# A macaron encoder trunk on one core: the first two weight units and x arrive in smaller pieces

## The reference

```python
def swiglu(x, w_gate, w_up, w_down):
    return (jax.nn.silu(x @ w_gate) * (x @ w_up)) @ w_down
...
    for l in range(DEPTH):
        x = layer_norm(ALPHA * x + FFN_RESIDUAL * swiglu(x, ffn1_w_gate[l], ffn1_w_up[l], ffn1_w_down[l]),
                       ln1_g[l], ln1_b[l])
        h = x @ w_in[l]
        ...
        x = layer_norm(ALPHA * x + mixed @ w_out[l], ln2_g[l], ln2_b[l])
        x = layer_norm(ALPHA * x + FFN_RESIDUAL * swiglu(x, ffn2_w_gate[l], ffn2_w_up[l], ffn2_w_down[l]),
                       ln3_g[l], ln3_b[l])
```

## Time and profile before

| | us |
|---|---|
| median of 3 runs | 986.75 |
| lowest and highest | 986.54, 987.31 |
| the profiled execution | 986.51 |
| its span, first to last instruction | 984.7 |
| PE matmul busy | 965.2 (98%) |
| DVE busy | 808.8 (82%) |
| ACT busy | 559.7 (57%) |
| mean granted TensorE clock | 0.997 |

### The profile page before, as it was taken

How to read it: one execution, slowest core, us unless ns; L and a number is a source line. 1 busy time by engine, 2 the same in 40 slices (tenths; PEclk the granted TensorE clock), 3 DMA queues, 4 the chain that set the end, 5 groups by cost and what they waited for, 6 DMA issues and landing times.

```text
span 984.7 us, 17315 instructions
## 1 busy us (share of the span) xinstructions
PE 965.2 (98%) x6744; PEld 892.4 (91%) x6744; DVE 808.8 (82%) x882; ACT 559.7 (57%) x611; POOL 21.1 (2%) x53
## 2 busy tenths in 40 slices
PE   6999999999999999999999999999999999999996
PEld 6999999899888999999989999998998889999996
DVE  5998887854888998887889988878469889988875
ACT  4655554557875655554565555544688656555543
POOL 1000000001000000000000000000010000000000
PEclk9999999999999999999999999999999999999998
DMA  8556645653244556454626684544624436645541
GB/s 332 215 207 243 240 171 172 214 214 129 92 162 156 201 202 226 171 215 172 239 80 221 213 298 171 213 172 171 214 87 164 152 155 214 226 169 216 173 154 43
DMA packets 33788, 184.14 MB, mean 187 GB/s; under 512 B 3792, under 2 KB 3792, under 8 KB 18640
## 3 DMA queue, kind: packets, MB, share of 16 engines
q1 hardware_dynamic: 32112, 173.55, 49.3%
q0 software_dynamic: 1488, 9.45, 2.3%
q10 hardware_dynamic: 144, 0.52, 0.1%
HBM read 182.46 MB, written 1.05 MB: 186 GB/s over the span
## 4 chain that ended last, share of the span: by engine, by line
PE 92%; DVE 5%; DMA 1%; ACT 1%; issue 0%; POOL 0%; DVEq 0%; SPq 0%; POOLq 0%
PE bank L1172 28%; PE bank L1173 28%; PE bank L1174 28%; PE bank L1301 7%; PE bank L1230 1%; DVE qT L869 1%; DVE soft_t L1058 1%; DMA raw<-stream 1%; PE bank L1484 1%; DVE xn L888 1%; DVE xT_lo L830 1%; DVE mx L1061 1%; DVE xn L856 1%; DVE w_lo L763 0%; DVE soft_t L1074 0%
## 5 line engine op out<-in xcount | busy, mean ns | idle before, releaser
L1172 PE MATMUL bank<-xT_hi,w_hi 128*128 128x256 f32 x1488 | 421.5, 283 | 0.0
L1174 PE MATMUL bank<-xT_hi,w_lo 128*128 128x256 f32 x1488 | 421.1, 283 | 0.0
L1173 PE MATMUL bank<-xT_lo,w_hi 128*128 128x256 f32 x1488 | 421.0, 283 | 0.0
L763 DVE TENSOR_TENSOR w_lo<-raw,w_hi 128x2048 fp32r<-128x2048 f32 x109 | 249.7, 2291 | 72.2 <-ACT w_hi L438 71.9
L438 ACT ACTIVATE w_hi<-raw 128x2048 fp32r<-128x2048 f32 x122 | 232.9, 1911 | 129.7 <-PE bank L1174 128.3
L1172 PEld LDWEIGHTS bank<-xT_hi,w_hi 128*128 128x128 f32 x1488 | 285.3, 192 | 3.9 <-issue 0.7
L1173 PEld LDWEIGHTS bank<-xT_lo,w_hi 128*128 128x128 f32 x1488 | 285.3, 192 | 3.0
L1174 PEld LDWEIGHTS bank<-xT_hi,w_lo 128*128 128x128 f32 x1488 | 285.3, 192 | 0.0
L1172 PE MATMUL bank<-w_hi,h_hi 128*128 128x512 f32 x284 | 111.4, 392 | 0.0
L1173 PE MATMUL bank<-w_lo,h_hi 128*128 128x512 f32 x284 | 111.4, 392 | 0.0
L1174 PE MATMUL bank<-w_hi,h_lo 128*128 128x512 f32 x284 | 110.5, 389 | 0.0
(11 more groups left out here) (151 smaller groups left out, 1197.4 us busy)
## 6 DMA issues: line engine op xcount, KB each, us to landing
raw<-stream SPq DMA_DIRECT2D x110, 1024.0 KB, 4.9
raw<-stream SPq DMA_DIRECT2D x108, 512.0 KB, 4.6
lnp<-ln_gb POOLq DMA_DIRECT2D x6, 1024.0 KB, 5.2
band<-rel_band POOLq DMA_DIRECT2D x2, 1024.0 KB, 9.1
xn<-x POOLq DMA_DIRECT2D x1, 1024.0 KB, 7.4
out<-xn SPq DMA_DIRECT2D x4, 256.0 KB, 2.0
qT<-xT SPq DMA_DIRECT2D x1, 512.0 KB, 4.9
qT<-xT ACTq DMA_DIRECT2D x1, 512.0 KB, 5.0
```

The source lines that it names most:

```text
L763: nc.vector.tensor_tensor(w_lo[:, at(slot)], raw[:, slot, :], w_hi[:, at(slot)].bitcast(F32), ALU.subtract).then_inc(lo_ready, 1)
L1172: nc.tensor.matmul(o, w[0], x[0], start=start, stop=False, skip_group_check=again)
L1173: nc.tensor.matmul(o, w[0], x[1], start=False, stop=False, skip_group_check=again)
L1174: return nc.tensor.matmul(o, w[1], x[0], start=False, stop=stop, skip_group_check=again)
```

## The change

Only the first two units of a layer's stream and the start of the program are edited.

- **Transfers.** SP no longer issues xT. It issues unit 0 as two quarters and a half (semaphores `quarter_ready`, `half_ready`, `raw_ready[0]`), and unit 1 as two halves (`u0_half_ready`, `raw_ready[1]`); this stands in the loop over layers, so it holds for both. ACT issues all of xT, as two quarters and a half, ahead of its table load.
- **Splitting.** ACT and DVE alternate between quarters of xT and of unit 0, then take unit 1 in halves, at the program's start. `first_hi` now counts three quarters and unit 1's first half there, so that the later phases wait for 4 where they waited for 1.
- **PE.** `first_two` replaces `first_columns` and the first `columns`: for each quarter of unit 0 and each half of unit 1 it runs high by high, low x, and low w. The count of real products is the same, 96. Before them, eleven products of the constant `neg_one` with itself (128x128, float32, into bank 3, which is overwritten later) run as soon as three constants are set.
- **A wait.** In the second feed-forward of layer 0, ACT waits for `quarter_ready` and `u0_half_ready` of the next layer before it splits that layer's unit 0.

```diff
-            sp.dma_start(qT[:, 0:4, :], xT_in[:, 0:4, :]).then_inc(xT_loaded[0], 16)
             sp.sem_inc(lo_ready, 3)
             with sp.Fori(0, DEPTH) as l:
-                for s in range(3):
-                    load(s, l * UNITS + s)
+                first = l * UNITS
+                sp.wait_ge(lo_ready, first + 1)
+                for c, ready in ((QUARTERS[0], quarter_ready), (QUARTERS[1], half_ready), (HALVES[1], raw_ready[0])):
+                    sp.dma_start(raw[:, 0, c], stream[first][:, c]).then_inc(ready, 16)
+                sp.wait_ge(lo_ready, first + 2)
+                for c, ready in zip(HALVES, (u0_half_ready, raw_ready[1])):
+                    sp.dma_start(raw[:, 1, c], stream[first + 1][:, c]).then_inc(ready, 16)
+                load(2, first + 2)
...
         def _(act):
+            for c, loaded_piece in zip((slice(0, 2), slice(2, 4), slice(4, 8)), xT_loaded):
+                act.dma_start(qT[:, c, :], xT_in[:, c, :]).then_inc(loaded_piece, 16)
             nc.scalar.preload_act_table(ACT.Silu)
             act.sem_inc(unit_used, 3)
-            act.dma_start(qT[:, 4:8, :], xT_in[:, 4:8, :]).then_inc(xT_loaded[1], 16)
...
                 if r < 3 * DEPTH - 2:
+                    if f == 1:
+                        act.wait_ge(quarter_ready, 16 * (l + 2))
+                        act.wait_ge(u0_half_ready, 16 * (l + 2))
                     split_hi(l, base + FFN_UNITS, 0, first[0] + FP, into=3, after=base + 3 * SF + 1)
...
+            for q, c in enumerate(QUARTERS):
+                part = slice(2 * q, 2 * q + 2)
+                act.wait_ge(xT_loaded[min(q, 2)], 16)
+                nc.scalar.activation(xT_hi[:, part, :], qT[:, part, :], ACT.Copy).then_inc(xhi_done, 1)
+                act.wait_ge((quarter_ready, half_ready, raw_ready[0], raw_ready[0])[q], 16)
+                nc.scalar.activation(w_hi[:, at(0, c)], raw[:, 0, c],
+                                     ACT.Copy).then_inc(hi_ready if q == 3 else first_hi, 1)
...
-                dve.wait_ge(first_hi, phase(l, p) + 1)
+                dve.wait_ge(first_hi, phase(l, p) + 4)
...
+                def all_three(slot, into, kcs, x_lo_at, w_lo_at):
+                    products(slot, into, kcs, w_hi, xT_hi)
+                    if x_lo_at:
+                        pe.wait_ge(xlo_done, x_lo_at)
+                    products(slot, into, kcs, w_hi, xT_lo)
+                    pe.wait_ge(*w_lo_at)
+                    return products(slot, into, kcs, w_lo, xT_hi)
+
+                for q in range(4):
+                    pe.wait_ge(xhi_done, q + 1)
+                    pe.wait_ge(*((hi_ready, 1) if q == 3 else (first_hi, q + 1)))
+                    last = all_three(0, bank[0], range(2 * q, 2 * q + 2), q + 1,
+                                     (lo_ready, split(0, 0)) if q == 3 else (first_lo, q + 1))
                 last.then_inc(unit_used, 1)
+                for half in range(2):
+                    pe.wait_ge(*((hi_ready, 2) if half else (first_hi, 4)))
+                    last = all_three(1, bank[7], range(4 * half, 4 * half + 4), 0,
+                                     (lo_ready, split(0, 1)) if half else (first_lo, 4))
+                last.then_inc(unit_used, 1)
...
+            def fill(count):
+                for i in range(count):
+                    plain(bank[3][:, 0:P], neg_one, neg_one, start=True, stop=True)
...
+            pe.wait_ge(consts, 3)
+            fill(11)
             pe.wait_ge(consts, 10)
```

65 lines of the change are left out of this document (26 added, 39 removed).

## The result

The changed kernel took **989.33 us** (median of 12 runs, 986.5 to 990.6) beside 986.75 of before (986.2 to 987.3 over 12 runs): a ratio of 1.0022, with a 95% interval of 1.0014 to 1.003. It is slower by 2.6 us by the medians and 2.2 by the ratio, where I forecast 1.1 us faster, and it lies outside my range. Its times also spread over 4 us, where before's spread over 1.

The account below looks back on a forecast made before the run. TensorE, nearly always busy and 92% of the last-ending chain, was taken as the bound. A 2.7 us gain at the start less 1.6 us lost at layer 0's end took 986.75 to 985.65, rounded to 985.6 us (range 983.9 to 987.3).

Parts of the forecast that it names:

- Unit 2's landing, PE at unit 2: Start: unit 2 lands at 14.8 us (14.1 to 15.8); PE starts on it at 19.1 instead of 22.65, 3.5 us earlier.
- The products of constants: Start: eleven constant products lie in PE's idle time and take the slow pace off real products; counted as nothing.
- What DVE can follow: First two steps: DVE's h_lo limits PE; old slack 1.76 plus 0.9 us earlier DVE run, lasting gain 2.7 (1.8 to 3.1).
- The wait at the layer's end: End of layer 0: ACT's split waits for the next unit 1's first half; PE gets hl_lo 1.6 us later (1.1 to 2.3).
- No slack but 0.1: End of layer 0: the chain from ACT's split through DVE to PE can absorb only 0.1 us of delay.
- Rival (b): Start: constants don't lift PE's clock, or pauses between quarters drop it again; 986.0 to 987.3 us, chance 0.08.
- (c): Start: pieces land late, x pushes unit 4 back, kernel slower; at least 1.6 us longer, 988.3, chance 0.13.

Follow-up runs that it names:

- kernel 5: Kernel with the pieces in layer 0 alone and neither added wait (984.42 us), without the eleven constant products at the start: 984.56 us, ratio 0.9976.
- Kernel 8: Kernel with the pieces in layer 0 alone (984.42 us), DVE's gate product and h sums moved ahead of unit 3's split: 983.33 us, then 983.83 again.
- kernel 11: Changed kernel with the next layer's unit 0 loaded in two halves, unit 1 still in halves, ACT waiting for unit 1's first half: 985.11 us, ratio 0.998.
- kernel 3: Before's start, with the changed kernel's pieces and both ACT waits at layer 0's end: 988.41 us, ratio 1.0021 to before.
- 6: Kernel with the pieces in layer 0 alone (984.42 us), plus ACT waiting for the whole next unit 1 before splitting the next unit 0: 985.89 us, ratio 0.999.
- 16: Changed kernel with layer 1's unit 0 loaded in four equal quarters ahead of unit 1's two halves: 987.32 us.
- kernel 13: Changed kernel, layer 1's unit 0 quarters replaced by upper and lower 64 partitions of its first half, in 4 KB rows: 988.68 us.
- the pair: Kernel with the pieces in layer 0 alone, ACT also waiting for the whole next unit 2, without and with constant products on PE meanwhile: 993.51 and 990.06 us.

## Why the prediction was wrong

- **Unit 2's landing, PE at unit 2.** Forecast 14.8 and 19.1. ACT's split of it started at 14.92 and PE was there at 19.48. The landing is right; PE's time is right in part by luck. Unit 2's low part was done at 16.87 + 2.29 = 19.16, and PE did not wait for it: from 9.33 on its own products follow each other without a gap until unit 1 ends at 19.48. I had them end at 18.7 and not stand in the way. The Trainium skill, page "DMA: Bandwidth & Descriptors" (Anatomy of one DMA), has its fixed part of about 2.0 us for transfers on gpsimd's path; here, on SP's queue, the one transfer more ahead of unit 2 came with 0.8 us (14.12 to 14.92).
- **The products of constants.** Taken at nothing: right, by kernel 5 even more than argued. The rule cited from the Trainium skill, page "TensorE: Matmul & The Clock Gate" (Part 1, What's actually happening), that activity releases the clock, agrees with the traces: behind the constants the real products start at full pace (0.12 us each from 6.81), and without them they start at 0.21.
- **What DVE can follow.** The mechanism was right: PE waits for h_lo, and the gain is the old slack of 1.76 plus what DVE's run moves. That was 0.65 us (41.87 to 41.22), not 0.9. DVE's run starts at 24.59, not 24.2, and without a wait for unit 4: DVE itself was not free, since unit 3's split started a microsecond later than before, and the gate's product stands behind it. Gain 2.2 instead of 2.7, inside the given 1.8 to 3.1. Kernel 8 takes that product out of the way.
- **The wait at the layer's end.** This is the step that failed. The mechanism, its place and those who wait were right; the size was not. I put the landing of the half at unit 0's landing plus 1.25 to 1.9 us, 480.3 to 481.0 in before's time and up to 0.5 later for the quarters, which is 478.1 to 479.3 with the faster start. It came at 480.9. With two halves ahead of it kernel 11 has it at 478.1, at the end I gave; I assumed that a third DMA ahead in the queue costs only its bytes. It cost up to 2.8 us, and scattered. The row I took the rate from was of whole units and two halves; no row had three pieces, and I gave this term no bound for that.
- **"No slack but 0.1".** The slack was 0.4 us. DVE, which takes up the split next, was itself that late with its queue: it waited 3.86 us where ACT waited 4.24.
- **The clock.** Rival (b) had it, but only for the start; I had the row that shows a clock at half after PE stopped and did not ask it of the wait that I forecast. By my 1.6 us of wait it would not have mattered: waits of that size brought none down (kernels 3, 6, 16). It came with the longer wait, 1.5 us.
- **Rivals.** (c) ends on the right side for the wrong place: pieces that land late, yet not at the start. Its range of time, 988.3 and more, holds the result, so that is luck. Its sum has a slip too: a gain of 0.3 against a loss of 1.6 is 1.3 us longer at least and not 1.6, so 988.05.

The sum with the measured terms is 2.2 - 3.8 - 1.5 = -3.1 us: 986.51 + 3.1 = 989.6, against 989.69 for the profiled execution.

## What to carry to other kernels

An engine that works in the order written holds up at a wait all that is queued behind it, so put the wait right ahead of the instruction that reads the data: here one line moved is 4.4 us, and the change turns from slower into 2 us faster. When a load is cut into pieces for one place in a loop, look at every other pass through the same code, and give a landing behind more DMAs than any row shows a bound of its own. When a forecast makes TensorE wait, ask whether its clock survives the wait.

## What was not expected of the hardware

- Three DMAs ahead of a transfer on one queue, with the same bytes as two, delayed its landing from 4.3 us (a whole unit from 4.9) to 6.5 to 7.1 in five of eight profiled executions (5.8, 5.2 and 4.8 in the others), with rows of 2 or 4 KB alike; with four, in one execution, it was 5.6. In the changed kernel the last four of the sixteen steps of its semaphore make 2 us of it. The times of kernels whose split waits for such a landing spread over 2 to 4 us, those of most others over about 1.
- With 3.2 to 3.7 us of idle TensorE the clock was at half for 3.4 us, nearly all of it products, 1.4 to 1.5 us of time; in kernel 13 an idle 3.0 us brought no fall. With 6.6 us of idleness it was low for longer (484.7 to 494.9), and cost 2.7 in the profiled execution and 3.4 by the medians of the pair.
- At the start the granted clock reads 1.00 while the spacing of products of 256 columns (0.21 us in kernel 5, and 0.12 from about 11.7 on) shows half. The traces' records of it begin at 4.4 to 7.0 us in the kernels with constants, at 11.66 in kernel 5, and at 13.62 and 14.29 in before and kernel 3.
